# DVE's gate products lag by four units, and inverse and transpose have semaphores of their own

## The reference

```python
A = L + jnp.eye(C)                      # L strictly lower, chunks of 64 tokens, 8 heads
sol = triangular_solve(A, rhs, lower=True, unit_diagonal=True)
...
def step(S, xs):                        # over the 8 chunks
    v_new = u_i - w_i @ S
    o = qd @ S + qk_i @ v_new
    S = S * exp(gl) + kd.T @ v_new
```

## Time and profile before

| | us |
|---|---|
| median of 3 runs | 2742.18 (2740.75 to 2745.46) |
| the profiled execution | 2751.09 |
| its span, on which all rows stand | 2749.1 |
| PE busy | 2558.3 (93% of the span) |
| DVE busy | 1451.3 (53%) |
| ScalarE busy | 1075.6 (39%) |
| POOL busy | 915.0 (33%) |
| DMA, mean over the span | 109 GB/s |
| mean granted clock of PE | 0.969 |

### The profile page before, as it was taken

How to read it: one execution, slowest core, us unless ns; L and a number is a source line. 1 busy time by engine, 2 the same in 40 slices (tenths; PEclk the granted TensorE clock), 3 DMA queues, 4 the chain that set the end, 5 groups by cost and what they waited for, 6 DMA issues and landing times. The chain is left out here.

```text
span 2749.1 us, 33369 instructions
## 1 busy us (share of the span) xinstructions
PE 2558.3 (93%) x13185; PEld 2054.3 (75%) x13185; DVE 1451.3 (53%) x2548; ACT 1075.6 (39%) x1872; POOL 915.0 (33%) x400
## 2 busy tenths in 40 slices
PE   5989998999989999989998989999999998999998
PEld 3767767897867888766776767877788886786787
DVE  6299649554645545545994562354444206736323
ACT  3445464245332332133554533543323223336432
POOL 1532232112434444335222221134344443332343
PEclk9999999899999999999999989999999998999999
DMA  7221325643233436532222153322223333831232
GB/s 252 63 71 53 123 69 155 179 138 131 92 112 133 143 102 206 179 116 66 73 76 97 51 119 89 122 89 92 77 93 106 94 98 112 153 115 51 73 122 77
DMA packets 331390, 300.00 MB, mean 109 GB/s; under 512 B 56718, under 2 KB 302820, under 8 KB 330212
## 3 DMA queue, kind: packets, MB, share of 16 engines
q1 hardware_dynamic: 279268, 279.52, 32.6%
q10 hardware_dynamic: 51968, 18.35, 2.6%
HBM read 267.92 MB, written 29.93 MB: 108 GB/s over the span
## 5 line engine op out<-in xcount | busy, mean ns | idle before, releaser
L275 PE MATMUL ps<-hh,split 128*128 128x512 f32 x3808 | 1289.0, 406 | 28.0 <-POOL split L222 17.3
L222 POOL TENSOR_TENSOR split<-ring,split 128x1024 fp32r<-128x1024 f32 (+2 forms) x340 | 808.1, 2378 | 1387.7 <-ACT split L218 1348.0
L275 PEld LDWEIGHTS ps<-hh,split 128*128 128x128 f32 x3808 | 727.3, 191 | 200.2 <-POOL split L222 31.3
L275 PE MATMUL ps<-hl,split 128*128 128x512 f32 x1904 | 752.1, 395 | 0.0
L218 ACT ACTIVATE split<-ring 128x1024 fp32r<-128x1024 f32 (+1 forms) x336 | 341.5, 1018 | 879.7 <-PE ps L275 678.3
L275 PEld LDWEIGHTS ps<-hl,split 128*128 128x128 f32 x1904 | 364.5, 191 | 73.1 <-issue 8.4
L275 PE MATMUL ps<-split 128*128 128x512 f32 x1152 | 283.9, 404 | 8.9 <-DVE split L1136 7.1
L275 PEld LDWEIGHTS ps<-split 128*128 128x128 f32 x1152 | 217.5, 189 | 70.3 <-issue 14.7
L2264 PE MATMUL ps<-split 128*128 128x512 f32 x1056 | 248.2, 397 | 0.0
L2264 PEld LDWEIGHTS ps<-split 128*128 128x128 f32 x1056 | 202.7, 192 | 42.8
L587 POOL TENSOR_TENSOR split<-ring,split 128x1024 fp32r<-128x1024 f32 x32 | 76.1, 2377 | 326.3 <-ACT split L579 326.3
(11 more groups left out here) (426 smaller groups left out, 3235.2 us busy)
## 6 DMA issues: line engine op xcount, KB each, us to landing
ring<-in_w_in_dram SPq DMA_DIRECT2D x60, 1024.0 KB, 5.2
ring<-in_w_up_dram SPq DMA_DIRECT2D x44, 1024.0 KB, 5.1
ring<-in_w_in_dram SPq DMA_DIRECT2D x34, 512.0 KB, 5.1
big<-in_w_ada_dram SPq DMA_DIRECT2D x16, 1024.0 KB, 8.5
ring<-in_w_ada_dram SPq DMA_DIRECT2D x32, 512.0 KB, 3.6
spare<-in_w_ada_dram SPq DMA_DIRECT2D x16, 1024.0 KB, 7.5
ring<-in_w_down_dram SPq DMA_DIRECT2D x16, 896.0 KB, 5.3
ring<-in_w_swa_out_dram SPq DMA_DIRECT2D x8, 1024.0 KB, 5.3
```

Of the source, the lines that this page charges most:

```text
L222: on.tensor_tensor(halves(pt, nk)[1], slot(n, nk)[:, :, e * P:(e + 1) * P], halves(pt, nk)[0], ALU.subtract).then_inc(low_made, 1)
L275: ins = nc.tensor.matmul(ps[bank[gt]][0:m, :], w[:, k, :], r[:, k, :], start=(k == 0 and w is w_high and r is rhs[0]), stop=(k == nk - 1 a ...
```

## The change

DVE's unit counter starts at -4 instead of 0, so each of its eight gate products is made four units later than before; the other engines' counters stay. The sends of the inverse and of its transpose get one semaphore each (`i_out[0]`, `i_out[1]`), and so do their fetches (`i_in[0][g]`, `i_in[1][g]`). On ScalarE the first fetch waits for the first send alone and the second for the second (plus a wait for `i_made` that is already met). On PE the first product of a pair waits for the inverse alone; the wait for the transpose comes after the level's products and fills.

```diff
-                    i_in = [sem(f"i_in{g}") for g in range(2)]
+                    i_out = [sem("i_out"), sem("it_out")]
+                    i_in = [[sem(f"{i}_in{g}") for g in range(2)] for i in ("i", "it")]
...
                                     if lv == 0:
-                                        pe.wait_ge(i_in[g], 32 * (pr + 1))
+                                        pe.wait_ge(i_in[0][g], 16 * (pr + 1))
...
                                     ins.then_inc(d_p, 1)
                                     fill(1)
+                                if lv == 0:
+                                    pe.wait_ge(i_in[1][g], 16 * (pr + 1))
                                 for e in range(2):
                                     c = 2 * pr + e
                                     pe.wait_ge(d_pc, at + e + 1)
...
-                            for a, away in ((sub_x, inv_away), (sub_xt, invt_away)):
+                            for a, away, out in ((sub_x, inv_away, i_out[0]), (sub_xt, invt_away, i_out[1])):
                                 nc.scalar.dma_start(diagonal(away, g), a[g].rearrange("p (r c) -> p r c", c=SUB)
-                                                    ).then_inc(i_out, 16)
+                                                    ).then_inc(out, 16)
 
                         def fetch_inverse(g, pr):
-                            if pr == 0:
-                                act.wait_ge(i_out, 32 * (g + 1))
-                            else:
+                            if pr:
                                 act.wait_ge(d_t, 6 * g + 6)
-                            for at, away in ((0, inv_away), (4, invt_away)):
+                            for n, (at, away) in enumerate(((0, inv_away), (4, invt_away))):
+                                if pr == 0:
+                                    act.wait_ge(i_out[n], 16 * (g + 1))
+                                if pr == 0 and n == 0:
+                                    act.wait_ge(i_made, g + 1)
                                 nc.scalar.dma_start(x[:, at + 2 * g:at + 2 * g + 2, :].rearrange("p a (h t) -> p (a h) t", h=4),
-                                                    whole(away, g, 8 * pr, 8)).then_inc(i_in[g], 16)
+                                                    whole(away, g, 8 * pr, 8)).then_inc(i_in[n][g], 16)
...
-                        done = added = open_ = 0
+                        done, added, open_ = -4, 0, 0
...
                                 done += 1
-                                if done % KD == 0:
+                                if done > 0 and done % KD == 0:
                                     served(done // KD - 1)
```

More of the change, by code:

```diff
@@ L1298, in build @@
                                                 "qk", "qd", "vturn"))
-                    l_out, l_in, i_made, i_step, i_out = (sem(s) for s in ("l_out", "l_in", "i_made", "i_step", "i_out"))
-                    i_in = [sem(f"i_in{g}") for g in range(2)]
+                    l_out, l_in, i_made, i_step = (sem(s) for s in ("l_out", "l_in", "i_made", "i_step"))
+                    i_out = [sem("i_out"), sem("it_out")]
+                    i_in = [[sem(f"{i}_in{g}") for g in range(2)] for i in ("i", "it")]
                     (d_p, d_pc, d_tp, d_t, d_tt, d_ttc) = (sem("d_" + s) for s in ("p", "pc", "tp", "t", "tt", "ttc"))
```

## The result

The changed kernel takes 2729.85 us (median of 5 runs, 2721.07 to 2733.10) against 2742.18 (5 runs, 2735.11 to 2745.46): ratio 0.9949, 95% interval 0.9928 to 0.9970. The forecast was 2732.0. The profiled execution of the changed kernel took 2721.07 us (span 2719.1), the lowest of its five runs, that of before 2751.09; their difference of 30 us says little. The mean granted clock is 0.979 in one and 0.969 in the other, and the five runs of the changed kernel alone spread over 12 us, the shorter ones at the higher clock. So the comparison has to be made stretch by stretch.

The account below looks back on a forecast made before the run. TensorE (PE), with work in 93% of the 2749.1 us span, was taken to bound the kernel. Gains of 3.9 + 0.7 + 5.5 = 10.1 us from 2742.18 gave 2732.0 us, range 2729 to 2735.5, stretched by rivals to 2723 and 2738.

Parts of the forecast that it names:

- two large terms: PE's gaps before the inverse's first level: gains of 3.9 us in layer 0 and 5.5 us in layer 1.
- The first fetch and PE's first wait: Before the inverse's first level: fetch and PE wait for the inverse alone, gaining 3.9 us (layer 0) and 5.5 (layer 1).
- longer by the overlap: Inverse's send: 3.1 us undisturbed plus its overlap with a weight tile's transfer; 4.2 us in layer 1, 4.9 in layer 0.
- The start of the inversion: DVE, layer 1: inversion of g = 0 starts 2.8 us sooner, of which 2.7 us arrives after POOL's split.
- The second wait and the mask: PE before the level's second half: transpose covered by 2.6 us (layer 0) and 1.5 (layer 1), layer 1's mask by 1.6.
- That would eat most of the gain: DVE, layer 1: without the lag it would stand for sigmoid 6, idle 1.53 us, costing most of the gain.
- L1504: PE's 1.1 us wait in layer 0, behind product 7 and DVE's additions: gain 0.7 us, between 0 and 1.1.
- The fall and a low stretch as now: PE's gaps: clock falls 3.8 us in, and the low stretch behind stays as before, adding nothing to the sum.
- 1: Rival, 20%: PE's clock is kept or returns sooner behind the gaps; 2727.3 us at half the low stretch, 2723.5 with none.
- 2: Rival, 14%: first fetch and second send, overlapped, share the DMA engines; gain only 5.7 us, 2736.5 us.
- 3: Rival, 6%: no effect; time is given back, or the early fetch blocks ScalarE's queue; 2741 to 2743 us.
- 4: Rival, 5%: slower; PE stays at low clock through all three levels of the first pair; 7.1 us slower, 2749.3 us.

Follow-up runs that it names:

- change_again: The changed kernel, unaltered, timed and profiled once more; ratio 0.9956 to the kernel before, 12 us faster.
- tile_held: The change, with SyncE holding the load of weight tile 8 until the inverse of g = 0 has been sent; ratio 0.9975 to the kernel before.
- own_lag: The change, with DVE's gate products 0 to 2 at their old place and only product 3 and later ones four units later; ratio 0.9949 to the kernel before.
- warm: The change, with 18 idle matmuls on PE filling the gap before the inverse's first level; ratio 0.9954 to the kernel before.
- sem_only: The change without the lag: own semaphores, DVE's counter from 0; ratio 0.9978 to the kernel before, 6 us faster.
- sem_warm: Own semaphores without the lag, with 19 idle matmuls in the gap; ratio 0.9992 to the kernel before.
- Before_warm: The kernel before, with 36 idle matmuls in the gap; ratio 0.9938 to the kernel before, and 0.9942 when repeated.
- both_waits: The change, but PE's first product waits for both fetches as before; ratio 0.9959 to the kernel before.
- lag_only: The kernel before with DVE's counter from -4, semaphores shared as before; ratio 0.9971 to the kernel before, 8 us faster.

## Why the prediction was right, point by point

The forecast of 2732.0 us against 2729.85, and 10.1 us of gain against 12 to 14, held, with the waits that it named. Its two large terms were each off by nearly 1 us in opposite directions, and that they cancelled is luck; what it left out, the shorter low stretch, is about what the total missed. One sum in it is wrong: the lower bounds of the three terms (3.9, 4.8 and 0) add up to 8.7 us, not 7.8. The forecast and its range don't hang on it.

*The first fetch and PE's first wait.* Right in mechanism, with 3.9 + 5.5 = 9.4 us forecast and 4.7 + 4.6 = 9.3 us in the profile (10.6 in change_again). The split is off: 4.7 and 4.6 us by the gaps where 3.9 and 5.5 were forecast. The step that failed is the size of the send, "longer by the overlap", which was taken from two rows. That such a send's landing goes with the tile's was right where much of the tile was left, as the table behind tile_held shows. But it then lands 1.5 us behind the tile; the row of before, 3.0 us behind it, was one of the seven slow ones. With 3.9 us instead of 4.9 for its send, layer 0 gained 0.8 us more than forecast. In layer 1 only 0.4 us of the tile was left, and the send took 4.5 us instead of 4.2; by the relation it would have been 3.1, so it too was slow for a reason that stays open. My bounds of 3.1 and 4.9 us held.

*The start of the inversion.* Mis-sized: 2.2 us instead of 2.8. I wrote that the lag on sigmoids 0 to 2 brings nothing; it costs, since product 2 now stands between the last two steps of the preparation, and own_lag got 0.55 us of it back. Two of POOL's splits fell into the inversion, and each stretched one step of 0.2 us to the whole instruction, as forecast for the first (2.44 and 2.40 us, beside splits of 2.41 and 2.40). The Trainium skill (SBUF — State Buffer, on the two sides of SBUF) has the pair of ports locked for a whole instruction, and the rows agree.

*The second wait and the mask.* Right: no gap before L1511 or L1515; in layer 1 the transpose lands 1.7 us before PE asks for it (forecast 1.5), in layer 0 2.5 us (forecast 2.6), and the mask is ready before it is needed. warm shows how narrow this is: at full clock both come late, by 0.7 and 1.6 us (forecast 0.9 for the mask). That DVE would otherwise stand for sigmoid 6 is shown by sem_only (1.7 us) and sem_warm (2.75). "That would eat most of the gain" was too strong at the low clock, where half of it stayed, and right at the full one.

*L1504.* 0.7 us forecast, 0.6 measured.

*The clock.* "The fall and a low stretch as now" was the weakest step. The fall was right: by the granted clock of 0.93 and 0.89 over the gaps it came 3.9 us into each (forecast 3.8). But the return varied: layer 0's level took 10.9 us in one profile of the same kernel and 14.0 in the next, layer 1's 10.4 and 10.7. In the profiled run the levels gave 2.2 + 1.0 us, which the sum didn't have, in the other -0.9 + 0.7. So the gaps are the steady 9 to 11 us of the gain in these two profiles, and the clock adds between 0 and 3.

*The rivals.* 1 happened in part (half the low stretch in layer 0 of the profile). 2 did not: fetches landed 4.1 us after their issue while the other send was under way; it is what a tile does to them (tile_held, 6.0 and 6.2 us). 3 and 4 did not happen. What comes nearest to 4, a second wait close behind the gap at which the clock falls, shows in layer 0 of sem_warm and of warm, though there the clock was back before the third level.

*What the local times leave out.* Before_warm (twice), both_waits, lag_only and own_lag are 3 to 7 us faster than their local times say. The granted clocks of all their runs show where. The low clock is half of full speed, so twice (1 - clock) times the span is the time spent at it: on the mean 153 us in the runs of before, 97 and 101 us in those of before_warm. That is 52 to 56 us less, but the gap and level of both layers held only 34 us of it in the profile of before, so some 20 us of low clock went elsewhere in the span. Among the runs of before themselves, 1 us less at the low clock goes with 0.4 to 0.45 us less time. By this estimate the 20 us are worth 8 to 9 us, where the local times miss 6 to 7. For both_waits and own_lag the same sum gives 17 and 14 us of low clock and 5 to 8 us of time, where 4 are missed. So this part is no matter of single profiles. Why a kernel spends less time at the low clock in stretches where its program is the same stays open.

## What to carry to other kernels

When an engine's gap is cut, list what it will ask for next and when each is ready at the speed it will then run at: here the semaphores alone brought 6 us, and with the mask freed by a lag of four units 12 to 14, because the second wait stood right behind the first. A gap on TensorE has two prices, its length and the low clock behind it; before shortening it with care, try to fill it, since 36 idle matmuls per gap in the untouched kernel gave 16 us, and halving the gaps on top of that gave nothing that could be told. And one duration of a DMA from one profile is a draw: two rows gave a wrong sum here, where 28 showed both a relation and its exceptions.

## What the runs showed of the hardware

- The low clock outlasted its cause. In before, PE was busy without a break for 11 us after each gap before the clock was back; the first levels, of short products, took 13.1 and 11.4 us where 8.3 and 6.7 are had at full clock. After gaps of 4.0 to 5.0 us they took 10.4 to 14.0 us, so the low stretch does not shrink in step with the gap. The Trainium skill (TensorE: Matmul & The Clock Gate, on the HAM clock gate) counts the ramp as under 1% of a typical kernel's span and advises against fitting a count of cold matmuls. The trace agrees with the size: two low stretches cost 9.0 and 9.5 us of levels, and the kernel without them took about 0.6% less time, twice. That is still as much as this change brings.
- A send of 128 KB took 3.1 to 5.1 us to land in the same place of the program (the table behind tile_held). The issue of the one behind it held ScalarE's queue for 0.93 to 2.84 us, in 27 of 28 cases 2.2 to 2.5 us less than the send took. The first fetch of 512 KB took 4.0 to 4.3 us, and 6.0 and 6.2 when a weight tile went out at the same moment (tile_held).
